# Rotary embedding of the retention heads moved from VectorE to GpSimd, with a swapped copy made by ScalarE

## The reference, cut to what matters

```python
def rope(x, pos):
    half = x.shape[-1] // 2
    ang = pos[:, None] * inv[None, :]
    x1, x2 = x[..., :half], x[..., half:]
    return concatenate([x1 * cos - x2 * sin, x2 * cos + x1 * sin], axis=-1)

q = rope(rq.reshape(B, T, H_RET, DK_RET), pos)                    # 8 heads of 128
k = rope(rk.reshape(B, T, H_RET, DK_RET), pos) * (DK_RET ** -0.5)
S_new, o_ret = retention_chunk(S, q, k, v)                        # decay tables, chunks of 128
```

## Time and profile before

| | |
|---|---|
| median of three runs | 2221.54 us |
| the profiled execution | 2221.23 us |
| its span in the profile | 2219.3 us |
| granted TensorE clock, mean | 0.989 |
| TensorE busy | 2133.4 us (96%) |
| VectorE busy | 1353.8 us (61%) |
| ScalarE busy | 789.3 us (36%) |
| GpSimd busy | 120.0 us (5%) |

### The profile page before, as it was taken

How to read it: one execution, slowest core, us unless ns; L and a number is a source line. 1 busy time by engine, 2 the same in 40 slices (tenths; PEclk the granted TensorE clock), 3 DMA queues, 4 the chain that set the end, 5 groups by cost and what they waited for, 6 DMA issues and landing times.

```text
span 2219.3 us, 42926 instructions
## 1 busy us (share of the span) xinstructions
PE 2133.4 (96%) x16152; PEld 2055.3 (93%) x16152; DVE 1353.8 (61%) x1809; ACT 789.3 (36%) x1124; POOL 120.0 (5%) x161
## 2 busy tenths in 40 slices
PE   5999999999999999999999999999999999999996
PEld 4999999999999999999989988999899999999996
DVE  4334443344356578888888888888887854442223
ACT  5334333343333444433333333333344532222223
POOL 4011110111010000000000000000000000000000
PEclk7999999999999999999999999999999999999998
DMA  4444444444334444424233333333346454443333
GB/s 143 133 128 134 132 117 119 123 141 126 110 93 134 137 124 124 130 69 133 89 108 103 105 108 109 117 108 107 106 132 197 124 159 146 140 147 108 97 106 128
DMA packets 454446, 271.74 MB, mean 122 GB/s; under 512 B 22498, under 2 KB 436450, under 8 KB 453090
## 3 DMA queue, kind: packets, MB, share of 16 engines
q1 hardware_dynamic: 452194, 265.99, 40.5%
q10 hardware_dynamic: 2176, 4.72, 0.5%
HBM read 232.89 MB, written 37.75 MB: 122 GB/s over the span
## 4 chain that ended last, share of the span: by engine, by line
PE 76%; DVE 11%; DVEq 7%; issue 3%; ACT 2%; POOL 1%; ACTq 0%; DMA 0%; SPq 0%; POOLq 0%
PE ACC L631 44%; PE ACC L862 14%; PE ACC L868 8%; PE Z L651 3%; DVE LO L1650 2%; DVEq L1667 2%; DVE RAW L1669 1%; DVEq L1799 1%; DVE RAW L1671 1%; ACT HI L1237 1%; PE Z L701 1%; DVE RAW L1666 1%; POOL XL L2008 1%; PE Z L777 1%; PE Z L715 1%
## 5 line engine op out<-in xcount | busy, mean ns | idle before, releaser
L1462 DVE TENSOR_TENSOR LO<-RAW,HI 128x512 fp32r<-128x512 f32 x304 | 212.8, 701 | 378.8 <-ACT HI L1075 358.6
L1237 ACT ACTIVATE HI<-RAW 128x1024 fp32r<-128x1024 f32 x266 | 272.4, 1054 | 407.6 <-PE ACC L868 243.8
L1650 DVE TENSOR_TENSOR LO<-RAW,HI 128x1024 fp32r<-128x1024 f32 x266 | 322.5, 1221 | 98.0 <-ACT HI L1237 87.4
L631 PE MATMUL ACC<-XH,HI 128*128 128x288 f32 x1664 | 367.6, 303 | 10.1 <-POOL XL L2008 6.5
L631 PE MATMUL ACC<-XH,LO 128*128 128x288 f32 x1664 | 357.6, 297 | 0.0
L631 PE MATMUL ACC<-XL,HI 128*128 128x288 f32 x1664 | 357.5, 297 | 0.0
L862 PE MATMUL ACC<-XH,HI 128*128 128x288 f32 x1216 | 329.9, 297 | 1.1 <-ACTq L1259 1.0
L862 PE MATMUL ACC<-XL,HI 128*128 128x288 f32 x1216 | 326.8, 295 | 0.0
L1075 ACT ACTIVATE HI<-RAW 128x512 fp32r<-128x512 f32 x304 | 190.3, 628 | 372.8 <-PE ACC L631 334.4
L631 PEld LDWEIGHTS ACC<-XH,HI 128*128 128x128 f32 x1664 | 267.5, 190 | 26.6 <-issue 15.0
L631 PEld LDWEIGHTS ACC<-XL,HI 128*128 128x128 f32 x1664 | 269.7, 190 | 0.0
(11 more groups left out here) (250 smaller groups left out, 2838.7 us busy)
## 6 DMA issues: line engine op xcount, KB each, us to landing
RAW<-in_w_in SPq DMA_DIRECT2D x224, 512.0 KB, 3.9
KC<-in_cache_sb_k SPq DMA_DIRECT2D x256, 64.0 KB, 1.9
VC<-in_cache_sb_v SPq DMA_DIRECT2D x256, 64.0 KB, 2.4
RAW<-in_w_ret_proj SPq DMA_DIRECT2D x32, 512.0 KB, 4.2
RAW<-in_w_out SPq DMA_DIRECT2D x32, 512.0 KB, 3.9
RAW<-in_w_sb_proj SPq DMA_DIRECT2D x16, 512.0 KB, 3.9
ST<-in_state_ret SPq DMA_DIRECT2D x64, 128.0 KB, 2.7
out<-ST SPq DMA_DIRECT2D x64, 128.0 KB, 3.4
```

Of the source, the lines that this page charges most:

```text
L631: mm = pe.matmul(ACC[a][:, half, 0:HALF], w[:, s // 2, s % 2 * QK + k, :], x[:, k0 + k, half * HALF:(half + 1) * HALF], start=first and k ...
L1237: act.activation(HI[:, SLOT[n]], RAW[:, SRC[n]], ACT.Copy).then_inc(S["hi_made"], 1)
L1462: dve.tensor_tensor(LO[:, s // 2, part, :], RAW[:, r, (n % 2) * QK:(n % 2 + 1) * QK, :], HI[:, s // 2, part, :].bitcast(F32), ALU.subtract ...
L1650: dve.tensor_tensor(LO[:, SLOT[n]], RAW[:, SRC[n]], HI[:, SLOT[n]].bitcast(F32), ALU.subtract)\
```

## The change

VectorE's `rotary` is gone. ScalarE copies RQK's two halves of partitions into the other halves of RTT at step 8, once the queries and keys are complete (`comb`), and signals `swapped`. GpSimd waits for TAB (`tab_in`) and `swapped`, multiplies RTT by the sine and RQK by the cosine, adds, signals `rot`, and goes on to QD and QM as before, after a new wait for the four `st_new` of the head before. The sign of the sine moves into the constant table.

```diff
@@ ScalarE
                 t.skip("sum_made", 4)
+                t.skip("comb", 7)
...
             def ret_new(n):
+                if n == 8:
+                    t.past("comb", 0)
+                    t.settle()
+                    for a, b in ((0, 64), (64, 0)):
+                        ins = act.activation(RTT[b:b + 64, :, :], RQK[a:a + 64, :, :], ACT.Copy)
+                    ins.then_inc(S["swapped"], 1)
@@ VectorE
-            def rotary(part):
-
-                if part < 2:
-                    a, b = ((0, 64), (64, 0))[part]
-                    dve.tensor_tensor(RTT[b:b + 64, :, :], RQK[a:a + 64, :, :],
-                                      one(RCS[a:a + 64, 1, :]).broadcast_to([64, 2, T]), ALU.mult)
-                if part == 2:
-                    dve.drain()
-                    dve.tensor_tensor(RQK[:, :, :], RQK[:, :, :], one(RCS[:, 0, :]).broadcast_to([P, 2, T]), ALU.mult)
-                    dve.drain()
-                if part == 3:
-                    dve.tensor_tensor(RQK[:, :, :], RQK[:, :, :], RTT[:, :, :], ALU.add).then_inc(S["rot"], 1)
...
             def ret_new(n):
-                if 10 <= n <= 13:
-                    rotary(n - 10)
@@ GpSimd
-            with pool.Fori(0, H) as i:
-                t.enter(i, 0, PER_RET)
+
+            def new_head(first):
                 t.take("tab_in", 16)
-                t.take("rot")
+                t.take("swapped")
+                sin = RCS[:, 1, :].rearrange("p (o n) -> p o n", o=1).broadcast_to([P, 2, T])
+                cos = RCS[:, 0, :].rearrange("p (o n) -> p o n", o=1).broadcast_to([P, 2, T])
+                pool.tensor_tensor(RTT[:, :, :], RTT[:, :, :], sin, ALU.mult)
+                pool.tensor_tensor(RQK[:, :, :], RQK[:, :, :], cos, ALU.mult)
+                pool.drain()
+                pool.tensor_tensor(RQK[:, :, :], RQK[:, :, :], RTT[:, :, :], ALU.add)
+                pool.drain().then_inc(S["rot"], 1)
+                if not first:
+                    t.take("st_new", 4)
+                    t.settle()
...
-                t.leave(H)
+
+            pool.wait_ge(S["rope_in"], 16)
+            new_head(True)
+            with pool.Fori(1, H) as i:
+                t.enter(i, 1, PER_RET)
+                new_head(False)
+                t.leave(H - 1)
...
-    rope[1] = np.concatenate([np.sin(ang), -np.sin(ang)])
+    rope[1] = np.concatenate([-np.sin(ang), np.sin(ang)])
```

More of the change, by code:

```diff
@@ L72 @@
     on=5, kd=1, qd=1, p_ready=2, km=4, s_ready=1, st_in0=64, st_in1=64, st_new=4, st_out0=64, st_out1=64, r_ready=1, r_out=16,
-    rvn=3, rot=1, tab_in=16, tab_used=1, gain_in=16, gain_used=1, s_out=16, gate_raw=2, ln_made=1, sig_made=1)
+    rvn=3, rot=1, tab_in=16, tab_used=1, gain_in=16, gain_used=1, s_out=16, gate_raw=2, ln_made=1, sig_made=1, swapped=1)
 PER_C = per(4, dve0=1, dve1=1, mg_in0=48, mg_in1=48, mg_used=2, t_ready=2, rh_done=2, merged=2)
```

## The result

| | before | after |
|---|---|---|
| median, us | 2221.24 (4 runs) | 2245.85 (4 runs) |
| span of the profiled execution, us | 2219.3 | 2244.5 |
| TensorE busy, us | 2133.4 | 2149.1 |
| TensorE idle (span less busy), us | 85.9 | 95.4 |
| granted TensorE clock, mean | 0.989 | 0.981 |

The ratio is 1.0114, 95% interval 1.0099 to 1.0129: 1.1% slower, where 2244 us was forecast. The same matmuls keep TensorE busy for 15.7 us more, and it idles for 9.5 us more. The first of these is in no term of the forecast.

A forecast was written before the change was run, and what follows sets the result against it. The prediction took the retention stage as bound by TensorE with VectorE just behind. Seven looped heads at 2.7 us plus 4.4 in the first give 23.3 us, added to 2221.2: 2244 us forecast, range 2225 to 2257.

The forecast's parts named there:

- The exclusion: A two-SBUF-operand VectorE instruction and a GpSimd instruction exclude each other, taking turns; three new GpSimd blocks of 2.6 us a head.
- Step 15: Looped heads: the 1.58 us HI stall goes, the LO stall grows by 1.2 us to near 2.8.
- the walk: The step-by-step forecast of a looped head: 1.2 us lost at step 15 plus 1.45 at step 1, about 2.7.
- The first head: At step 10 TensorE waits for a late LO until 942.5: 4.4 us, bounds 2 and 6.
- the wait grows by 1.45: At step 1 of the next head, TensorE's 1.40 us wait for VectorE's LO grows by 1.45 us.
- The sum: Seven looped heads at 2.7 us plus 4.4 us in the first head: 23.3 us slower.
- the relief wins: Rival: VectorE's instructions slip between GpSimd's, both step 15 stalls go, late step 9 stays: -12.9 us, 2208; chance 0.13.
- Half is absorbed: Rival: VectorE's lag is made up before step 20; step 15 and first-head losses stay: 13 us, 2234; chance 0.24.

The follow-up runs named there:

- e1: The changed kernel with GpSimd's three rotation instructions a head cut into six of 576 elements: 2227.4 us, ratio 1.0035 to the kernel before.
- e5: The changed kernel with ScalarE's copies at step 10 and GpSimd rotating without waiting for the head's table (waits only before QD): 2249.2 us, ratio 1.0130 to before.
- e2: The changed kernel with ScalarE's swapped copies at step 10 in place of step 8: 2230.3 us, ratio 1.0038 to the kernel before.
- e6: As e5, with GpSimd's rotation also cut into the six shorter instructions of e1: 2214.8 us, ratio 0.9975 to the kernel before.
- e3: The kernel before, rotation on VectorE, with the LO of step 15 made twice: 2237.7 us, ratio 1.0079.
- e4: The kernel before, rotation on VectorE, with the LO of step 15 made three times: 2253.3 us, ratio 1.0153.
- e9: Kernel before with ScalarE's copies at step 10, VectorE rotating in three instructions, GpSimd's QD and QM behind step 17's value copies: 2204.8 us, ratio 0.9931.

## Why the prediction was right, and where it was not

The number was right, its direction and its cause (GpSimd's instructions block VectorE where VectorE is late) too. One term of the sum was wrong, and another effect of nearly its size stood in its place; that the sum came so close is luck to that extent.

- **The exclusion** was forecast rightly. A block has the full length of the GpSimd instruction, and the engines take turns; e1 and e5 show it. The cosine product takes 2.5 us net where 2.6 was taken, and the first head's sine product, which found VectorE idle, was recorded at 2.68. The Trainium skill's rule (page "SBUF — State Buffer", section "Who interferes with whom": the loser blocks for the whole instruction) agrees with the trace. So, nearly, does its figure of about 2.5 cycles an element for two inputs (page "GPSIMD Engine Reference", section "Instruction dispatch"), by which 2.4 us is the estimate, for 2.5 measured.
- **Step 15**: step 9 was forecast late by 0.9 us and was by 0.82; the HI stall of step 15 went; the LO stall, "near 2.8", was 2.88. Together the head's idle time grew by 0.96 us; the walk had 1.2. TensorE did not wait for `rot`: the sum ended at 1497.77, `query_key` began at 1505.51.
- **The first head**: TensorE was forecast to resume at 942.5 and did at 942.45; the stall is 3.71 us where 4.4 was priced. The whole head lost more: step 1 of the next head moved from 983.21 to 989.87, 6.7 us, because the clock fell here as well: TensorE was busy for 3.0 us more up to there (109.63 for 106.62).
- **The wrong step**: "the wait grows by 1.45" at step 1. It did not grow (1.40 and 1.41). In its place the clock fell at step 15, and TensorE was busy for 1.36 us more in the head shown, and 13.2 us more in all seven (590.19 for 577.02), where 7 x 1.45 = 10.2 us of waiting had been forecast. The two are linked, as e2 shows: with the clock up VectorE's lag does arrive at step 1, but as 0.67 us, not 1.45; e1's heads with the clock up show 1.54 for 1.40. As an estimate from these, stalls alone would have given 7 x (0.96 + 0.1 to 0.7) + 3.7 = 11 to 15 us. The span grew by 25.2 us, and 15.7 of these are busy time. So some three fifths of the loss are the clock, which the prediction put at nothing: it read a clock of 1.00 and took it as given, while it forecast longer idle times.
- **The sum**: seven looped heads took 625.86 us from the first step 1 to the last (rows below, after), and 606.04 before: 19.8 us longer for 18.9 forecast; the first head 6.7 for 4.4; behind the heads 1.3 us came back. Of the 19.8 only 6.65 us are idle time, where all 18.9 had been forecast as such.

```profile
989.87 1.33 PE L868 MATMUL ACC<-TH,LO 128*128 128x288 f32 x8 [1.50 <-DVE LO L1657]
...
1615.73 1.32 PE L868 MATMUL ACC<-TH,LO 128*128 128x288 f32 x8 [1.24 <-DVE LO L1657]
```

The same two before:

```profile
983.21 1.33 PE L868 MATMUL ACC<-TH,LO 128*128 128x288 f32 x8 [1.50 <-DVE LO L1650]
...
1589.25 1.33 PE L868 MATMUL ACC<-TH,LO 128*128 128x288 f32 x8 [1.23 <-DVE LO L1650]
```

The busy time of all seven looped heads together, after and before:

```profile
989.87:1615.73 625.86, 590.19 (x4166) 559.11 (x4166) 523.16 (x722) 216.67 (x267) 89.87 (x35) 0.98 0.35 104
```

```profile
983.21:1589.25 606.04, 577.02 (x4166) 546.30 (x4166) 521.19 (x750) 200.44 (x253) 21.29 (x14) 1.00 0.36 107
```

- **The rivals**: "the relief wins" was to decide from blocks under about 1 us; e6, with blocks of about 1.2 us and the early place, is that case and is in fact faster than before. "Half is absorbed" (2234) would, by the estimate above, have been nearly right for the stalls without the clock.

What stays open is which stalls let the clock fall. In the looped heads the stall of step 15 did it in four of seven at 1.8 us (e1), in five of seven at 2.4 to 2.5 us (e3), in three of seven at 2.9 us (e2), and in all seven at 2.9 us in the changed kernel, where a stall at step 9 comes before it, and at 3.7 to 3.8 us in e4. Stalls of 1.9 to 2.1 us at step 1 did it four times in e2, and those of 4.4 us at step 10 seven times in e5. Stalls of 1.1 to 1.6 us never did, nor did one of 1.8 us for HI in the kernel before and one of 2.5 us in e4's first head. So the length of the stall alone does not decide, and the runs do not say what does.

## What to carry to other kernels

Before moving elementwise work from VectorE to GpSimd, price it as a block of its full length (2.2 ns an element here) on every VectorE instruction beside it that has both operands in SBUF, and not as work off the path. Cut it into pieces no longer than VectorE's own instructions (e1, e6), and place it where no urgent VectorE instruction stands behind it (e9); idle time of VectorE nearby is not enough (e5). When a forecast lengthens TensorE's stalls where the clock stood at its full level, price a fall too: here 1.3 to 1.6 us where the clock was low for 3.4 us, and 2.7 to 3.0 us where it was low for 6.8. Half a change can be the good half: the copies on ScalarE, placed behind the urgent instruction, with the rotation left on VectorE, beat both kernels.

## What the runs showed of the hardware

- A VectorE instruction of 0.42 us waited its turn behind a GpSimd instruction of about 2.5 us and lasted 2.88 (e5). Instructions with one operand in PSUM kept their length beside GpSimd; in the changed kernel these two ran inside the cosine product (1490.57 to 1494.19, its wait until 1491.68 included):

```profile
1491.61 0.44 DVE L1663 TENSOR_TENSOR RVT<-RVT,ACC 128x288 f32<-128x288 f32 x1
1491.98 0.44 DVE L1665 TENSOR_TENSOR RVT<-RVT,ACC 128x288 f32<-128x288 f32 x1
```

- A stall of TensorE of 2.9 us in the changed kernel, made by GpSimd's blocks, went with 3.4 or 6.8 us at the lower clock level, and so did one of 3.7 to 3.8 us in e4, made by repeated VectorE work.
- ScalarE's copy of 64 x 1152 was no faster than its activation of 128 x 1152 (1.16 us): two took 2.35 us.
